# Gate and up of an fp32r SwiGLU FFN with stationary weights, hidden product kept by features

## The reference

```python
def rms_norm(x, g):
    xf = x.astype(jnp.float32)
    y = xf * lax.rsqrt(jnp.mean(xf * xf, axis=-1, keepdims=True) + EPS)
    return (y * g.astype(jnp.float32)).astype(x.dtype)

def swiglu(x, w_gu, w_down):
    gate, up = jnp.split(x @ w_gu, 2, axis=-1)
    return (jax.nn.silu(gate) * up) @ w_down

x = x + 0.5 * swiglu(rms_norm(x, ffn1_norm[l]), ffn1_w_gu[l], ffn1_w_down[l])
```

## Time and profile before

| | us |
|---|---|
| median of 3 runs | 3350.33 (3346.92 to 3353.32) |
| the profiled execution: its time | 3347.18 |
| its span, first to last instruction | 3345.4 |
| mean granted TensorE clock in it | 0.934 |
| TensorE busy in it | 3006.6 (90%) |
| VectorE busy | 1800.5 (54%) |
| ScalarE busy | 1471.2 (44%) |
| HBM traffic | 145 GB/s over the span |

### The profile page before, as it was taken

How to read it: one execution, slowest core, us unless ns; L and a number is a source line. 1 busy time by engine, 2 the same in 40 slices (tenths; PEclk the granted TensorE clock), 3 DMA queues, 4 the chain that set the end, 5 groups by cost and what they waited for, 6 DMA issues and landing times. The chain is left out here.

```text
span 3345.4 us, 37979 instructions
## 1 busy us (share of the span) xinstructions
PE 3006.6 (90%) x15764; PEld 2526.8 (76%) x15764; DVE 1800.5 (54%) x2493; ACT 1471.2 (44%) x2046; POOL 16.3 (0%) x21
## 2 busy tenths in 40 slices
PE   4998688997997999998897698999999799999799
PEld 4888686886785688787797597787879688888687
DVE  3558364554554555545557635646554555555654
ACT  4544212554443454443444343444454354544544
POOL 0000000000000000000000100000000000000000
PEclk8999786997998899999998788999999899999899
DMA  4554100553453155554344043554555355554453
GB/s 157 176 189 152 63 1 25 188 178 108 163 179 115 57 180 185 189 179 149 113 154 151 1 152 126 181 183 161 179 176 165 125 178 187 176 186 134 165 185 130
DMA packets 371919, 488.66 MB, mean 146 GB/s; under 512 B 17103, under 2 KB 331044, under 8 KB 371620
## 3 DMA queue, kind: packets, MB, share of 16 engines
q1 hardware_dynamic: 371410, 486.11, 44.5%
q10 hardware_dynamic: 338, 0.13, 0.0%
HBM read 485.14 MB, written 1.05 MB: 145 GB/s over the span
## 5 line engine op out<-in xcount | busy, mean ns | idle before, releaser
L221 DVE TENSOR_TENSOR weights_lo<-weights_raw,weights_hi 128x2048 fp32r<-128x2048 f32 (+2 forms) x282 | 629.5, 2236 | 499.2 <-ACT weights_hi L204 498.9
L226 DVE SCALAR_TENSOR_TENSOR weights_lo<-weights_raw,params,weights_hi 128x512 fp32r<-128x512 f32 (+1 forms) x736 | 492.9, 733 | 467.6 <-ACT weights_hi L208 467.5
L816 PE MATMUL work<-weights_hi,input_hi 128*128 128x512 f32 x1760 | 708.9, 403 | 12.2 <-PEq L148 6.8
L817 PE MATMUL work<-weights_lo,input_hi 128*128 128x512 f32 x1760 | 697.6, 396 | 0.0
L818 PE MATMUL work<-weights_hi,input_lo 128*128 128x512 f32 x1760 | 697.0, 396 | 0.0
L208 ACT ACTIVATE weights_hi<-weights_raw,params 128x512 fp32r<-128x512 f32 (+1 forms) x736 | 462.9, 701 | 363.3 <-DMA weights_raw<-in_ffn_w_in 179.5
L204 ACT ACTIVATE weights_hi<-weights_raw 128x2048 fp32r<-128x2048 f32 (+2 forms) x282 | 525.4, 1865 | 157.1 <-DMA weights_raw<-in_ffn_w_up 89.5
L816 PEld LDWEIGHTS work<-weights_hi,input_hi 128*128 128x128 f32 x1760 | 332.5, 189 | 88.2 <-DVE input_lo L378 7.0
L818 PEld LDWEIGHTS work<-weights_hi,input_lo 128*128 128x128 f32 x1760 | 332.0, 189 | 80.6
L817 PEld LDWEIGHTS work<-weights_lo,input_hi 128*128 128x128 f32 x1760 | 332.7, 189 | 74.7
L246 PE MATMUL work<-input_hi,weights_hi 128*128 128x256 f32 (+2 forms) x1160 | 333.8, 288 | 47.1 <-PEq L148 25.0
(11 more groups left out here) (413 smaller groups left out, 3225.2 us busy)
## 6 DMA issues: line engine op xcount, KB each, us to landing
weights_raw<-in_ffn_w_gu SPq DMA_DIRECT2D x176, 512.0 KB, 4.7
weights_raw<-in_ffn_w_in SPq DMA_DIRECT2D x176, 512.0 KB, 4.6
weights_raw<-in_ffn_w_down SPq DMA_DIRECT2D x66, 1024.0 KB, 4.9
weights_raw<-in_w_in SPq DMA_DIRECT2D x44, 1024.0 KB, 5.1
weights_raw<-in_ffn_w_out SPq DMA_DIRECT2D x44, 1024.0 KB, 4.8
weights_raw<-in_a_w_in SPq DMA_DIRECT2D x29, 1024.0 KB, 5.7
weights_raw<-in_ffn_w_gate SPq DMA_DIRECT2D x44, 512.0 KB, 3.7
weights_raw<-in_ffn_w_up SPq DMA_DIRECT2D x44, 512.0 KB, 4.7
```

What stands on the lines that cost most here:

```text
L221: last = self.nc.vector.tensor_tensor(self.wl[:, n % SLOTS, 0:kc * cols], raw, self.wh[:, n % SLOTS, 0:kc * cols].bitcast(F32), ALU.subtract)
L226: last = self.nc.vector.scalar_tensor_tensor(out=lo[:, k, :], in0=raw[:, k * cols:(k + 1) * cols], scalar=g[:, gain[1] + k:gain[1] + k + 1 ...
L816: nc.tensor.matmul(o, K.hi[:, c, ts], wh[:, k, :], start=(c == 0), stop=False)
L817: nc.tensor.matmul(o, K.hi[:, c, ts], wl[:, k, :], start=False, stop=False)
```

## The change

In `ffn`, gate and up now have 128 weight columns stationary and all 256 tokens moving (`part`), as the projections do. The results lie by features: gate in one bank, up in another, two blocks of 128 features by 256 tokens. The product `hidden` has features on partitions and goes into the down projection without transposes. The inverse root varies along the free axis now, so the gate is multiplied by the root as a row (`gate_r`) on VectorE before the silu; up isn't scaled, and its root comes in with the factor 0.5 at the residual add (`half`), where tokens are partitions again. The whole step's silu, product, rounding and splitting are single 128x512 operations. Step 0 takes its input as the mixers do (`before_chunk`), BY_HALVES or, behind a layer norm, BY_TOKENS, and the normed FFNs make the row of roots.

```diff
-    def add_quarter(self, dve, i, q, base, last_item, alpha, out_scale):
+    def add_quarter(self, dve, i, q, base, last_item, alpha, scale_of):
...
-        if out_scale != 1.0:
-            ins = self.nc.vector.scalar_tensor_tensor(out=xq, in0=y, scalar=out_scale, in1=xq, op0=ALU.mult, op1=ALU.add)
+        if scale_of:
+            ins = self.nc.vector.scalar_tensor_tensor(out=xq, in0=y, scalar=scale_of(t), in1=xq, op0=ALU.mult, op1=ALU.add)
...
             dve.wait_ge(*K.rooted(self.norm_n + 1))
             nc.vector.reciprocal(self.rcol, K.root[:, NT:2 * NT]).then_inc(*K.inverse.up())
+            dve.wait_ge(*K.inverse(self.norm_n + 1))
+            nc.vector.tensor_scalar(K.half[:, :], self.rcol, 0.5, None, ALU.mult).then_inc(*K.halved.up())
         if self.row:
-            dve.wait_ge(*K.inverse(self.norm_n + 1))
             nc.vector.tensor_tensor(K.diag[:, :, :], K.c("ident").unsqueeze(1).to_broadcast([P, NT, P]),
                                     self.rcol.unsqueeze(2).to_broadcast([P, NT, P]), ALU.mult).then_inc(*K.spread.up())
 
...
 def ffn(K, feed, tail, alpha=1.0, join=True):
     nc, norm = K.nc, feed.norm
...
         with K.stage(3 * NF, join=join) as (block, n0):
...
+            gate_bank = lambda s: K.work[:, 2 * (s % 2), :]
+            up_bank = lambda s: K.work[:, 2 * (s % 2) + 1, :]
...
             def _(sp):
...
             @block.tensor
             def _(pe):
...
+                def part(bank, n, c0, w0, before=None):
                     wh, wl = K.item(n)
...
+                    for m in range(2):
+                        o, ms = bank[:, m * T:(m + 1) * T], slice(w0 + m * P, w0 + (m + 1) * P)
+                        for k in range(4):
+                            if before and m == 0:
+                                before(pe, c0 + k)
+                            c = c0 + k
+                            nc.tensor.matmul(o, wh[:, k, ms], K.hi[:, c, :], start=(c == 0 and m == 0), stop=False,
+                                             skip_group_check=True)
+                            nc.tensor.matmul(o, wh[:, k, ms], K.lo[:, c, :], start=False, stop=False, skip_group_check=True)
+                            last = nc.tensor.matmul(o, wl[:, k, ms], K.hi[:, c, :], start=False, stop=(c == DC - 1),
+                                                    skip_group_check=True)
                     return last
...
                 def pair(s):
                     return hh[:, s % 2, :, :], hl[:, s % 2, :, :]
...
                 for s in range(NF):
...
+                    before = feed.before_chunk if s == 0 else None
+                    K.arrived(pe, a_item(s))
+                    if s >= 2:
+                        pe.wait_ge(*(gscaled if norm else silued)(s - 1))
+                    part(gate_bank(s), a_item(s), 0, 0, before)
+                    if s >= 2:
+                        pe.wait_ge(*hidden(s - 1))
+                    part(up_bank(s), a_item(s), 0, FSTEP).then_inc(K.used, 1)
+                    if s == 0:
+                        feed.sum_row(pe)
+                    K.arrived(pe, b_item(s))
+                    part(gate_bank(s), b_item(s), 4, 0, before).then_inc(*gated.up())
+                    part(up_bank(s), b_item(s), 4, FSTEP).then_inc(K.used, 1)
                     if 0 < s < LAST:
...
                         pe.wait_ge(*hsplit(s))
                         K.arrived(pe, down_item(s - 1))
                         for q in BY_TOKENS:
                             last = K.quarter(pe, down_item(s - 1), pair(s - 1), q, s == 1, False)
                         last.then_inc(K.used, 1)
...
                 def before(j):
...
+                    if j in (0, 2):
+                        pe.wait_ge(*hsplit(LAST + j // 2))
                 K.last_rows(pe, down_item(LAST - 1), (pair(LAST - 1), pair(LAST)), tail, before)
...
             @block.scalar
             def _(act):
+                feed.copy_row(act)
                 for s in range(NF):
...
+                    if norm:
+                        act.wait_ge(*gscaled(s + 1))
+                    else:
+                        act.wait_ge(*gated(s + 1))
+                    if s >= 2:
+                        act.wait_ge(*hidden(s - 1))
+                    nc.scalar.activation(sg[:, s % 2, :, :], gr[:, s % 2, :, :] if norm else two(gate_bank(s)), ACT.Silu)\
+                        .then_inc(*silued.up())
                     K.round_weights(act, a_item(s) + 1 + LEAD)
...
+                    act.wait_ge(*hidden(s + 1))
+                    if s >= 2:
+                        act.wait_ge(K.used, down_item(s - 2) + 1)
+                    nc.scalar.activation(hh[:, s % 2, :, :], hid[:, s % 2, :, :], ACT.Copy).then_inc(*hrounded.up())
                     K.round_weights(act, b_item(s) + 1 + LEAD)
...
                     if s == 1 and alpha != 1.0:
...
                         nc.scalar.activation(K.x[:, :, :], K.x[:, :, :], ACT.Copy, scale=alpha).then_inc(*K.scaled.up())
...
+                    if 0 < s < LAST:
+                        K.round_weights(act, down_item(s - 1) + 1 + LEAD)
                 tail.scalar_part(act)
...
             @block.vector
             def _(dve):
+                feed.await_row(dve)
                 for s in range(NF):
+                    if norm:
+                        dve.wait_ge(*gated(s + 1))
+                        if s >= 2:
+                            dve.wait_ge(*silued(s - 1))
+                        nc.vector.tensor_tensor(gr[:, s % 2, :, :], two(gate_bank(s)),
+                                                K.rstd[:, 0:T].unsqueeze(1).to_broadcast([P, 2, T]), ALU.mult)\
+                            .then_inc(*gscaled.up())
                     K.split_weights(dve, a_item(s) + 1 + LEAD)
...
+                    dve.wait_ge(*silued(s + 1))
+                    dve.wait_ge(K.used, b_item(s) + 1)
+                    if s >= 2:
+                        dve.wait_ge(*hsplit(s - 1))
+                    nc.vector.tensor_tensor(hid[:, s % 2, :, :], sg[:, s % 2, :, :], two(up_bank(s)), ALU.mult)\
+                        .then_inc(*hidden.up())
+                    if s < LAST:
+                        K.split_weights(dve, b_item(s) + 1 + LEAD)
+                    dve.wait_ge(*hrounded(s + 1))
+                    nc.vector.tensor_tensor(hl[:, s % 2, :, :], hid[:, s % 2, :, :], hh[:, s % 2, :, :].bitcast(F32),
+                                            ALU.subtract).then_inc(*hsplit.up())
                     if 0 < s < LAST:
                         K.split_weights(dve, down_item(s - 1) + 1 + LEAD)
...
                 if alpha != 1.0:
                     dve.wait_ge(*K.scaled(K.scaled.sent))
...
+                feed.await_half(dve)
+                tail.vector_part(dve, down_item(LAST), 1.0, lambda t: K.half[:, t:t + 1] if norm else 0.5)
...
-        def next_ffn():
-            return Feed(K, K.x, BY_TOKENS, norm=True)
+        def next_ffn(order=BY_HALVES):
+            return Feed(K, K.x, order, norm=True, row=True)
...
             mix, second = mixer(None), next_ffn()
+            latent.row = False
             ffn(K, latent, FeedTail(K, mix), join=False)
...
-        first = next_ffn()
+        first = next_ffn(BY_TOKENS)
         ffn(K, plain[2], NormTail(K, first, A["ln3_g_2"], A["ln3_b_2"]), alpha=ALPHA)
```

More of the change, by code:

```diff
@@ L412, in inverse_ready, with await_half @@
         return self.K.inverse(self.norm_n + 1)
+    def await_half(self, dve):
+        if self.norm:
+            dve.wait_ge(*self.K.halved(self.norm_n + 1))
     def sum_row(self, pe):
@@ L998, in _ @@
                     K.split_weights(dve, n0 + i + 1 + LEAD)
-            tail.vector_part(dve, n0 + items - 1, alpha, 1.0)
+            tail.vector_part(dve, n0 + items - 1, alpha, None)
 def project_features(K, src, chunks, dst, pair=None):
```

128 lines of the change are left out of this document (13 added, 115 removed).

## The result

The changed kernel took **3366.1 us** (median of 5 runs, 3360.7 to 3368.0), the kernel before 3348.0 beside it (3345.8 to 3353.3): ratio 1.005, 95% interval 1.0039 to 1.0062. It is slower by 0.5%, not by the 1.1% that was forecast.

The account below looks back on a forecast made before the run. TensorE's queue was taken as the bound, with nothing waiting inside a step. The terms -32 + 10 - 4 + 22 + 10 + 6 + 22 + 4 gave +38 us on 3347.2, on the median 3388, stated as 3387 us; range 3356 to 3418.

Parts of the forecast that it names:

- The steps: Steady FFN steps: 11.33 us of gate and up plus 5.60 of down, 16.93 instead of 17.22; ten FFNs gain 32 us.
- The transposes: In each FFN step the four transposes go, 0.42 us a step, 4.6 us per FFN.
- First steps: Start of the 8 normed FFNs: less cover makes TensorE wait for item b of step 2, 1.3 us each, +10 us.
- The ring: Steady steps: VectorE's and ScalarE's chain of gate work and weight splits becomes the bound, +33 us, 3420; 10%.
- rival 2: The ring of VectorE and ScalarE becomes the bound in the steps: +33 us, 3420; 10%.
- rival 3: Gate and up: weight loads pace the matmuls, 18.2 us a step for 11.3, 760 us in all, 4110; 2%.
- The last step: Each FFN's last step: TensorE stalls for the hidden product, 2.4 us in 8 normed and 1.6 in 2 plain FFNs, +22.
- 4 us of clock for three longer gaps: Starts behind a layer norm: the granted clock falls in longer gaps in three places, 4 us (0 to 8).
- Tails and row: FFN ends: two weight splits delay the residual adds, +10; four FFN starts: the row's matmul waits for the diagonals, +6.
- Layer-norm starts: Three FFNs and the hybrid mixer: all of step 0 waits for the second token tile, extra split delays the norm, +22.
- the +4: Longer gaps at three places behind layer norms let the granted clock fall: 4 us (0 to 8).
- rival 1: Edges between FFNs are covered: weight splits in VectorE's chain find cover, 49 us go, 3338, half covered about 3362; 16%.

Follow-up runs that it names:

- run 5: The kernel before with one unused tile of 32 bytes a partition ahead of root_diagonals: 3330.0 us, ratio 0.9944.
- run 6: The changed kernel with one more unused tile of 32 bytes ahead of root_diagonals: 3368.0 us, ratio 1.0063 to the kernel before.
- run 2: The changed kernel with extra matmuls that nobody reads (9, plain FFNs 6) filling TensorE's wait in the last step: 3358.1 us.
- run 1: The changed kernel with the last down item rounded before ScalarE waits for the scaled gate, in each FFN's last step: 3330.3 us.
- run 12: The changed kernel with the first step of the three FFNs behind a layer norm run by token tiles, in 128-column matmuls: 3417.2 us.
- run 4: The changed kernel with its five FFN tiles allocated in another order, hidden_hi and hidden_lo 8 KB nearer: 3361.0 us, ratio 1.0045 to the kernel before.

## Why the prediction was off

**The steps: this failed.** The prediction put "96 x 0.118 = 11.33 us" beside "48 x 0.233 = 11.20", and "a step takes 11.33 + 5.60 = 16.93". Measured are 11.20 + 5.46 = 16.66. Over 90 steps the first term was 12 us too dear and the second another 13. The 0.118 came from 21 spacings of one projection, used to three digits as if it were the price of the form. A longer look at the same trace would have given less: another projection of the kernel before has 750 spacings from 1728.07 to 1815.57 us, 0.1167 each, which is what gate and up then took. Over the placements the form measured 0.1167 to 0.120 in gate and up. And the 5.60 was taken over as unchanged, since the diff doesn't touch the down matmuls; but it adds an 8-byte tile, which moves hidden_hi from offset 96 to 128 within 256 bytes, the residue of the weights. That the tile's shift did it is shown by run 5 (the kernel before gains 18 us by the same shift) and run 6 (the changed kernel's pace goes back). The transposes (-0.42 a step) were right.

Where both kernels have the same placement, run 5 and the changed kernel, the difference is 36 us. The structural part of the forecast, +38, was thus near; the measured change was that and a gain of 18 that came with the tile. This is partly luck, since the terms inside it were off in both directions: between these two kernels steps 1 to 9 gain 33 us and not 20, and the last steps lose 13 us of clock that the forecast didn't have.

**First steps** (+10): step 2 is 0.9 us longer in the eight normed FFNs, 7.5 us; TensorE waits for the split there (4.8). **The ring** (rival 2) did not become the bound: a constant period of 16.67. Loads don't pace the matmuls (rival 3): by the Trainium skill, page "TensorE: Matmul & The Clock Gate", section "Back-to-back issue gap", the estimate was 98 ns at 256 columns against 131 at 512; the trace has 117 and 227 to 233, and the measurement decides.

**The last step** (+22): the wait is 19.6, mechanism and size right. Its consequence was missed: the granted clock fell behind an idle time of 2.1 us. The forecast had 4 us of clock for three longer gaps and none here. Run 2 shows 12.9 us of clock in these steps, and run 1 that one rounding's place was worth 36 us in all.

**Tails and row** (+10, +6): the turns wait 8.7 us for x, where the kernel before shows no such wait, and the row's matmul waits 1.8 in place of four times 1.1. **Layer-norm starts** (+22, and the +4): from run 1, without the stall, the three parts that hold them grew by 7.9, 11.1 and 12.2 us against the kernel before (forecast 6.4, 5.5 and 2.3, and 8.0), 31 in all, and the changed kernel has the clock at 0.50 from 1356 to 1365 at the first, where the kernel before has 1.00 throughout (PE busy, clock, DMA share, GB/s):

```profile
1356.00:1359.00 3.00, 0.00 (x0) 0.50 0.00 0
1359.00:1362.00 3.00, 1.97 (x8) 0.50 0.48 167
1362.00:1365.00 3.00, 2.85 (x13) 0.50 0.59 183
```

The timelines separate most of the 31. Up to the FFN's first gate matmul TensorE is idle 7.9, 9.2 and 14.0 us in the three starts of run 1, and 1.0, 1.2 and 2.9 in the kernel before: 26 us are waiting, the longest piece of it each time for the second tile (5.9, 8.3 and 8.2), for which the kernel before waits 1.0 to 2.5 us inside its step 0. At most 5 are left for the clock there and for the hybrid mixer. The edges were thus not covered (rival 1), though run 1 shows that a change of order could cover more than half of them, and then the changed kernel is even with the one before at the same placement (3330 against 3330 in run 5).

## What to carry to other kernels

Before an unchanged instruction is costed at its old duration, look at whether the change moves its operands: a tile of a few bytes shifts all that is allocated behind it, and here that was worth as much as the whole measured effect, with the opposite sign. Compare forms of a matmul at several placements: of those tried here, the best for one form was the worst for the other. Read the granted clock beside every spacing before it is called the price of a form: in run 12 the same matmul took 0.112 and 0.213 us. A chain that ends 2 us late can cost more than 2 us if the engine that waits is TensorE; ask first whether independent work (here one rounding) only stands in the wrong place of the order.

## What the runs showed of the hardware that was not expected

- The spacing of identical fp32r matmuls at full clock depends on where the operands start: 0.227 to 0.228 us with 512 moving columns where stationary and moving operand start at the same residue of 256 bytes, 0.232 to 0.2335 at the others tried; with 256 columns 0.120 at equal residues and 0.1167 at 32 bytes apart. It repeats from step to step, and the fast down stream was seen on four chips. Why was not found. The weights always stood 128 past a multiple of 256, so equality as such is not shown. Nor is the residue all: with one and the same placement, projections of the kernel before took 0.1167 in one stream and 0.118 in another. The Trainium skill, page "SBUF — State Buffer", section "Operand start alignment", states which starts are legal and says that its runs timed nothing; these do.
- 128 moving columns took 0.112 us at the full clock, against 0.117 for 256; at 0.50 they took 0.213 (run 12).
- The granted clock fell towards 0.50 behind 2.11 us of idle time in all eight normed FFNs of the changed kernel and in six of eight in run 4; behind 2.06 in four of eight in run 6. In none of these three kernels did it fall in the two plain FFNs, with 1.30 and 1.35 us of idle time. Behind the gap after the second FFN it was back within 6 us of work in one kernel (0.60, then 1.00) and stayed at 0.50 through 12 us more of full work in two others, which differ from it by the place of one instruction group; in run 12 it stayed at 0.50 through 45 us of nearly full work.
